# Decayed sample states of the SSD mixer: from two GpSimd products to sixteen ScalarE activations per group

## What is computed

```
decay_to_end = jnp.exp(cum[:, :, -1:] - cum)
chunk_states = einsum('bcsgn,bcsgh,bcsghp->bcghpn', Bc, decay_to_end, x)
chunk_decay  = jnp.exp(cum[:, :, -1])
def step(s, inp):
    dec, st = inp
    return dec[..., None, None] * s + st, s      # new state = decay * old state + st
y_off = einsum('bcqgn,bcghpn,bcqgh->bcqghp', Cc, s_prev, exp(cum))
```

## Time and profile before

| | us |
|---|---|
| median of 3 runs | 1008.92 |
| the 3 runs | 1009.87, 1002.57, 1008.92 |
| profiled execution | 1002.44 |
| its span, first to last instruction | 1000.6 |

### The profile page before, as it was taken

How to read it: one execution, slowest core, us unless ns; L and a number is a source line. 1 busy time by engine, 2 the same in 40 slices (tenths; PEclk the granted TensorE clock), 3 DMA queues, 4 the chain that set the end, 5 groups by cost and what they waited for, 6 DMA issues and landing times.

```text
span 1000.6 us, 16530 instructions
## 1 busy us (share of the span) xinstructions
PE 899.4 (90%) x5345; PEld 681.3 (68%) x5345; DVE 585.7 (59%) x1092; ACT 414.8 (41%) x713; POOL 168.3 (17%) x214
## 2 busy tenths in 40 slices
PE   6589999989889998998969999989999999999986
PEld 3388879878787887888849997774444444444464
DVE  2786777788787778878785542434333242423534
ACT  2457565655746565465764321351111111111232
POOL 0045233241513324152400000020000000000000
PEclk9889898989979898999959999998999999999998
DMA  7154462727346272734637513935999999999201
GB/s 202 43 134 127 112 179 63 194 74 204 81 117 179 54 204 69 199 84 126 173 108 198 165 39 109 385 148 193 382 391 380 383 388 392 379 389 376 65 1 47
DMA packets 208603, 188.54 MB, mean 188 GB/s; under 512 B 8000, under 2 KB 166392, under 8 KB 208568
## 3 DMA queue, kind: packets, MB, share of 16 engines
q1 hardware_dynamic: 207352, 187.12, 58.5%
q10 hardware_dynamic: 1216, 0.98, 0.4%
HBM read 176.88 MB, written 11.21 MB: 188 GB/s over the span
## 4 chain that ended last, share of the span: by engine, by line
PE 59%; DVE 17%; issue 12%; ACT 7%; POOL 2%; DVEq 1%; DMA 1%; POOLq 0%; SPq 0%; ACTq 0%
PE bank L1768 12%; PE bank L1796 6%; PE bank L1724 6%; PE bank L1632 5%; PE bank L1731 4%; PE bank L1465 3%; PE bank L1661 3%; PE bank L1467 3%; PE bank L1466 3%; PE bank L1816 3%; PE bank L1636 2%; DVE wlo L1008 2%; DVE cv L1075 2%; PE bank L1538 2%; DVE arena L1193 1%
## 5 line engine op out<-in xcount | busy, mean ns | idle before, releaser
L1465 PE MATMUL bank<-h_hi,whi 128*128 128x288 f32 x640 | 203.9, 319 | 20.8 <-DVE wlo L1008 20.6
L1466 PE MATMUL bank<-h_lo,whi 128*128 128x288 f32 x640 | 196.0, 306 | 0.0
L1467 PE MATMUL bank<-h_hi,wlo 128*128 128x288 f32 x640 | 195.1, 305 | 0.0
L1465 PEld LDWEIGHTS bank<-h_hi,whi 128*128 128x128 f32 x640 | 127.6, 199 | 32.4 <-DVE wlo L1008 27.2
L1362 DVE TENSOR_TENSOR xT<-xT,bank 128x288 f32<-128x288 f32 x128 | 49.6, 449 | 152.3 <-PE bank L1731 152.3
L1466 PEld LDWEIGHTS bank<-h_lo,whi 128*128 128x128 f32 x640 | 127.6, 199 | 1.0
L1467 PEld LDWEIGHTS bank<-h_hi,wlo 128*128 128x128 f32 x640 | 127.4, 199 | 0.0
L722 ACT ACTIVATE whi<-wb 128x1024 fp32r<-128x1024 f32 x82 | 86.9, 1060 | 91.1 <-PE bank L1467 79.2
L1008 DVE TENSOR_TENSOR wlo<-wb,whi 128x1024 fp32r<-128x1024 f32 x82 | 108.0, 1318 | 23.0 <-ACT whi L722 16.0
L936 ACT ACTIVATE Gs<-bank 128x512 f32<-128x512 f32 x16 | 9.6, 597 | 144.8 <-PE bank L1768 144.8
L1724 PE MATMUL bank<-pick,htok 96*128 96x256 f32 x240 | 59.0, 386 | 1.1 <-ACT yb L915 1.1
(11 more groups left out here) (368 smaller groups left out, 1564.9 us busy)
## 6 DMA issues: line engine op xcount, KB each, us to landing
wb<-in_w SPq DMA_DIRECT2D x80, 1024.0 KB, 8.4
wb<-in_w_in SPq DMA_DIRECT2D x80, 512.0 KB, 4.0
wb3a<-in_w SPq DMA_DIRECT2D x16, 1024.0 KB, 8.6
arena<-in_state_ssd SPq DMA_DIRECT2D x16, 512.0 KB, 5.7
out_new_ssd_s<-arena SPq DMA_DIRECT2D x16, 512.0 KB, 5.9
wb<-in_w_br_ssd SPq DMA_DIRECT2D x16, 512.0 KB, 3.9
wb<-in_w_br_lru SPq DMA_DIRECT2D x8, 512.0 KB, 4.0
wb<-in_w_out SPq DMA_DIRECT2D x8, 512.0 KB, 4.0
```

The lines of the kernel that those rows point to most:

```text
L1465: mm(bP[i % 2][:, 0:T], hi, h_hi[:, k, :], start=(k == 0), stop=False)
L1466: mm(bP[i % 2][:, 0:T], hi, h_lo[:, k, :], start=False, stop=False)
L1467: ins = mm(bP[i % 2][:, 0:T], lo, h_hi[:, k, :], start=False, stop=(k == KC - 1))
```

## The change

ScalarE makes the decayed states, with a function `decay_states(j)` of eight activations: one for each sample, of 128 partitions by 128 numbers, function Identity, whose scale is a column of `ex` (one factor for each partition). It stands twice in ScalarE's list, ahead of `from_T(7)` and behind it. Pool's two products and their waits are gone. The semaphore `sdec_ready` counts 16 for each group where it counted 2, and VectorE waits for 8 and 16.

```diff
-        sdec_ready = sig("sdec_ready", 2)
+        sdec_ready = sig("sdec_ready", 2 * NB)
@@ Pool, end of its loop body
-                pool.wait_ge(CU_free.sem, CU_free.at(g, 3))
-                for j in range(2):
-                    pool.wait_ge(sin_landed, g * 32 + 32)
-                    if j == 0:
-                        pool.wait_ge(state_out, g * 48 + 1)
-                    dec = ex[:, j, P + NT - 1:P + NS:NT]
-                    ch.tell(eng.tensor_tensor(Snew[:, j], Sin[:, j], dec.unsqueeze(2).to_broadcast([P, NB, P]), ALU.mult), sdec_ready, j + 1)
@@ ScalarE, in group()
+                def decay_states(j):
+                    act.wait_ge(sin_landed, g * 32 + 32)
+                    act.wait_ge(state_out, g * 48 + 1)
+                    for b in range(NB):
+                        act_f(Snew[:, j, b, :], Sin[:, j, b, :], ACT.Identity,
+                              scale=ex[:, j, P + NT * b + NT - 1:P + NT * b + NT]).then_inc(sdec_ready.sem, 1)
@@
                 raw(9, gb[:, ds(g, 1), :].rearrange("p o t -> p (o t)"))
+                decay_states(0)
                 from_T(7, sT[:, 0:4, :].rearrange("p b n -> p (b n)"), 512)
+                decay_states(1)
                 if not last:
                     evac(g, 10)
@@ VectorE, new_states(k)
-                    dve.wait_ge(sdec_ready.sem, sdec_ready.at(g, j + 1))
+                    dve.wait_ge(sdec_ready.sem, sdec_ready.at(g, NB * (j + 1)))
```

## The result

| | before | changed |
|---|---|---|
| median, 20 runs each | 1005.31 us | 1012.41 us |
| lowest and highest | 1000.74, 1010.95 | 1007.85, 1017.77 |
| profiled execution's span | 1000.6 us | 1006.8 us |

The changed kernel takes 1.0074 times as long, 95% interval 1.0057 to 1.0091: 7.4 us more (the two medians differ by 7.1), within 1%. The three runs of before that the prediction had seen had a median of 1008.92; over 20 runs it is 1005.31. That lifts the forecast of 1021 by 3.6 us beyond what its sum added.

The account below looks back on a forecast made before the run. The prediction took VectorE's chain to L1197 as the bound, with ScalarE's `from_T(8)` and TensorE's `y_state(1)` nearly as long beside it. 9.4 us of lateness plus 3 of clock made 12, on 1009: 1021 us, range 1008 to 1033.

Parts of the forecast that it names:

- the cover behind `from_T(8)`: ScalarE's 2.04 us of idle around GELU, its table loads and the square, said to absorb the 1.59 us delay.
- Pool's relief: Without Pool's products VectorE is ready for L1197 about 2.8 us sooner, 1.7 if L645 holds up `small` 11.
- The rival on the other side: L1197 follows VectorE's own chain: 2.8 us back in six groups, 17 us faster, 992 us; chance 0.04.
- the first term of the sum: Lateness of `from_T(8)` on ScalarE, less VectorE's lead at L1197, over eight groups: 9.4 us.
- The price and the register waits: ScalarE ahead of `from_T(8)`: 0.312 us an activation, 0.17 us per pair of waits, less idle and lead: 9.4 us.
- TensorE's clock: Longer idle ahead of `y_state(1)` brings the low clock more often: 1.2 us a group, 3 us in all, bounds 0 and 7.
- The extra cover of group 4: 2.16 us of ScalarE idle ahead of `from_T(7)`, 1.09 us more cover, so a delay of only 0.65 us there.
- The baseline: Time the loss was added to: 1009 us, from the 1008.92 us median of three runs of the kernel before.
- The covered case: ScalarE's idle covers sixteen activations at 0.21 us each, 3.4 us against 3.6 of idle: 1007 us; chance 0.10.
- the clock: Rival: TensorE's clock falls no earlier than now, so 9.4 us of loss, 1018 us, within 1%; chance 0.25.
- a costly row: Rival: ScalarE's activations cost 0.405 us each in a row, 12 us more, 1033 us; chance 0.18.
- The covered rival: The scale tile costs nothing in a row, so ScalarE's idle covers the sixteen activations: 1007 us; chance 0.10.

Follow-up runs that it names:

- the Pool part alone: Kernel before without Pool's two products: nobody makes the decayed states, VectorE adds PSUM to the old state, ScalarE's list unchanged; 1002.14 us, ratio 0.9966.

## Why the prediction came out as it did

**The direction, the place and the mechanism held.** The price of sixteen activations was more than the idle ahead of `from_T(8)`; the first eight's delay of `from_T(7)` cost nothing; the cover behind `from_T(8)` held (1.20 us of idle were left ahead of the square); Pool's relief came back on VectorE, 2.4 us in a group of the loop, with `small` 11 held up as I had allowed for, and ended as a wait at L1199, in all eight groups, of 2.8 to 4.7 us where I had said 1.5 or more; and the parts behind did not take the delay back, but for 1.4 us, the larger part of which looks like the clock's. The rival on the other side, that Pool's hold was the whole price, fell: the Pool part alone is worth 3.4 us, of which the forecast had 1.2 us in each of groups 2 and 3.

**The size was wrong.** The sum said 12 us; the runs said 7.4, within 1%. The step that failed is the first term of the sum, the lateness of `from_T(8)`, priced at 9.4 us from 0.312 us an activation and 0.17 us for each pair of waits: it measured 5.5. I had given slower by over 1% a chance of 0.56 and within 1% only 0.38. 1012.41 lies inside the range of 1008 to 1033. These terms of the sum were off:

- *The price and the register waits*: 9.4 us forecast, 5.5 in the table. In each loop group the forecast delay of `from_T(8)` was 1.74, 0.65 or 1.15 us; measured were 1.22, 0.13 and 0.62: 0.52 less every time. Of it 0.27 is the step from start to start, 0.295 us and not 0.312 (16 x 0.017); 0.18 are the register waits, 0.12 us ahead of the first eight (211.93 to 212.05) and 0.04 ahead of the second where I had taken 0.17 twice; the rest are small pieces, such as `from_T(7)` with 0.57 us and not 0.60. Each is a tenth of the sixteen's price or less. But the delay is what is left of 5 us over 3.6 us of idle, and 0.5 off a remainder of 1.7 is a third of it. Six groups make 3.1 us; groups 0 and 7, forecast 1.3 and 2.1, were 0.94 and 1.74, another 0.7.
- *TensorE's clock*: 3 us forecast, 1.9 in the profile. `y_state(1)` took longer in groups 0, 2, 3, 6 and 7, as long in 4, and shorter in 1 and 5. In group 5, where it had been 3.15, it was 2.12. I had treated the low clock as fixed to its group; it isn't. The extra cover of group 4 was such a stretch too: the granted clock was 0.57 from 324.5 to 328.5 us, ahead of the 2.16 us of idle. In the loop's groups of the profiles read here the length goes with the idle ahead: 1.95 to 2.19 behind 1.60 to 1.90 us, but for one of 3.15 in the kernel before; 2.12 to 3.21 behind 2.28 to 2.83; 3.57 or 3.58 behind 4.75 and more. Group 0 of the changed kernel doesn't fit the middle class, with 3.58 behind 2.60. No run took the clock away by itself, so this term is read from the profiles and not shown by an experiment.
- *The baseline*: 1009 for a kernel whose median is 1005.3.

Two readings were off without weight in the sum. Pool's first product in group 2 took 2.22 us and not the mean of 2.07, so the first long L1096 ended 0.33 us behind it, not 0.5. The covered case came to 1007, and the range began at 1008.

**The chances.** My rivals took the idle, the clock and a costly row each at its full size, and none was "the mechanism as forecast, each term a little smaller". With three terms that all could only be taken from neighbours, and a forecast 2 us over the 1% line, within 1% deserved at least as much as slower.

The covered rival had its arithmetic right: with a constant scale the step is 0.202 us, and the run with it gave 0.997. Its condition, that the tile costs nothing in a row, is what failed. The Trainium skill (ScalarE: Activation LUTs, What ACT_TABLE_LOAD costs) states 93 ns for each pointer operand and an overlap of 93 ns between neighbours; the prediction's estimate from its figures was 0.29 us from start to start. The trace agrees, 0.295; I had set that estimate beside a higher one from this kernel's rows, and it was the closer of the two.

## What to carry to other kernels

Work moved to an engine is priced by what its next consumer waits for, not by its busy share: ScalarE is busy 45% and the same eight activations a group cost 11 us in one slot, where it was already full, and nothing some 6 us later, behind the last thing that `y_state(1)` needs of ScalarE. Where the cost is what spills over an idle gap, write the range from the error of the price times the number of gaps, for the remainder carries the whole error. And a stall taken off an engine is worth only its lead over the second chain to the same instruction: 1.2 of 2.4 us in groups 2 and 3 here.

## What the hardware showed that I had not expected

- **An order of starts 0.1 us apart went with 0.65% of the kernel's time.** With Pool's product 0.03 us ahead of VectorE's pair, both of the pair and a cast were held (2.20, 1.72, 3.04 us); with it 0.06 behind, one of the pair and the scan (0.52, 1.72, 2.36). The kernels differ by one wait that is already met: 1.014 against 1.0075. Some of it can be the clock's, as said above.
- **In a row of activations with a scale tile the ends overlap as in one with a constant**: 0.389 long, 0.295 apart; with a constant 0.296 long, 0.202 apart. The overlap is 0.094 in both.
- **The low stretches of TensorE's clock move between groups from one execution to the next**: 0.66 in group 2 of the changed kernel where it was 1.00 before. `large` 11 came up to 1.0 us earlier or later in single groups, by 0.1 in the sum over eight.
